# The order of VectorE's state updates and row statistics in the inner cell of an mLSTM step

## The chip, the cores and the metric

The kernel runs on one core of a Trainium2 chip. The metric is the device time of one execution in microseconds. It was run three times as it stood before; the median is 2390.78 us (2387.2 to 2397.85).

## The reference

One step of a two-layer decoder: layer 0 is sliding-window attention, layer 1 an mLSTM block in chunkwise form. The change touches only the chunkwise cell of layer 1, for one head and one chunk of the prompt:

```python
def step(carry, xs):
    C, n, m = carry                       # C (512, 512) per head
    ...
    s = jnp.einsum('bthd,bjhd->btjh', qc, kc) * w_intra
    num = jnp.einsum('btjh,bjhd->bthd', s, vc) + w_inter[..., None] * jnp.einsum('bthd,bhde->bthe', qc, C)
    den = jnp.sum(s, axis=2) + w_inter * jnp.einsum('bthd,bhd->bth', qc, n)
    h = num / jnp.maximum(jnp.abs(den), jnp.exp(-m_t))[..., None]
    ...
    C_new = decay[..., None, None] * C + jnp.einsum('bjhd,bjhe->bhde', kc * wk[..., None], vc)
# after the scan, per token and head:
mu = jnp.mean(h_cell, axis=-1, keepdims=True)
var = jnp.mean(jnp.square(h_cell - mu), axis=-1, keepdims=True)
h_norm = (h_cell - mu) * lax.rsqrt(var + EPS)
```

There are 4 heads of width 512. The prompt has 16 + 1024 tokens, which this kernel cuts into one chunk of 16 and eight of 128 rows. A sample group of 8 sequences with 4 tokens each goes through the same cell as a tenth chunk, and each sequence has a 512 x 512 state of its own.

## The kernel before

The program is written engine by engine: each engine has its own list of instructions in a fixed order, and semaphores hold the lists together. The work of one head in the cell is written by `cell_sp`, `cell_gp`, `cell_pe`, `cell_act` and `cell_dve`. The helper `heads` writes head 0 and head 3 out and runs heads 1 and 2 as two turns of a hardware loop, in which some waits compare with a register. So the same source line has slightly other spacings in heads 1 and 2 than in heads 0 and 3.

For each prompt chunk c (0 to 8) TensorE does, in this order (`cell_pe`):

1. the numerator: queries times the old state C (L1635), a one-column product for the denominator (L1638) and, interleaved with them from chunk 2 on, the four state products of one sample sequence (L1591); then scores times values (L1641, L1646); it then signals `small_ready`;
2. the four 128 x 512 tiles of the new state's product K^T V, three matmuls each (L1653). They go to two PSUM banks in turn, so tile 0 and tile 1 can be made at once, tile 2 waits until VectorE has taken tile 0 into the state (`c_done`), and tile 3 until it has taken tile 1;
3. transposes of the next chunk's keys and values and the next scores (`pre(c + 1)`: L1564, L1570), and a sample numerator (L1601);
4. `back(c)`: the transposes of the normalised output `hb` (L1582), which wait for `h_done(c)` from VectorE. The next chunk's numerator stands behind them and also waits for `sw_done(c + 1)`, VectorE's product of the next scores and weights (L1796).

VectorE (`cell_dve`) does, from `small_ready` on: the denominator (L1943, L1853 to L1855), two state updates, the row statistics of the numerator (`statistics`: L1860, L1861, L1862, the last of which signals `var`), the other two state updates (L1872; L1870 in chunk 0), `normed` (L1879, L1880), which signals `h_done`, the next scores (L1796) and a small update. ScalarE turns the variance into 1/sqrt in two small operations (`norm`: L1745, L1747) and then converts the next chunk's keys and values (`turned`: L1722, L1724). `normed` waits for the second of the small operations (`h_rstd`). These are the functions in question:

```python
done(dve.bn_stats(x[:, 2:8], numerator(c)))                      # statistics(c)
done(dve.bn_aggr(x[:, 8:10], x[:, 2:8]))
dve.tensor_scalar(x[:, 10:11], x[:, 9:10], x[:, 1:2], x[:, 1:2], ALU.mult, ALU.mult).then_inc(sem("var"), 1)
...
dve.wait_ge(sem("u_ready"), due(NU * h + u + 1))                 # prompt_state(c, k)
ins = dve.scalar_tensor_tensor(cst[:, k, :], cst[:, k, :], hbc[:, 1, c:c + 1], U, ALU.mult, ALU.add)
ins.then_inc(sem("c_done"), 1)
...
dve.wait_ge(sem("h_rstd"), due(NCH * h + c + 1))                 # normed(c)
```

In chunk 8 there is no next chunk: after its tiles TensorE does a sample numerator and the four state products of the last sample sequence (L1591), of which the third waits for a VectorE update (L1811) that stands behind `normed(8)` and a copy (L1956). Behind them come `back(8)`, VectorE's gating (L1890), GpSimd's and ScalarE's part of it (L1506, L1752, L1513), and then the output projection (L1678).

Of the kernel before, what the change touches and what calls it, by code (L numbers as in the profile page):

```python
# [97 lines left out]
def due(n):  # L98

    n = n.v if isinstance(n, Idx) else n  # L100
    return max(n, 0) if isinstance(n, int) else n
# [31 lines left out]
def build(nc, a, o):  # L133
# [3 lines left out]
    def sem(name):  # L137
        if name not in sems:
            sems[name] = nc.alloc_semaphore(name + sem_suffix[0])
        return sems[name]  # L140
# [1172 lines left out]
    def u_tile(c, k):  # L1313

        return 4 * c + k if c < 2 else 8 * c - 4 + k
# [465 lines left out]
    def cell_dve(dve, h):  # L1781
        step = [0]

        def done(ins):

            ins.then_inc(sem("cell_step"), 1)
            step[0] += 1
            wait_apart(dve, sem("cell_step"), CELL_STEPS * h + step[0])

        def scores(c):  # L1790
            n, r = ROWN[c], c % 2
            W = sws if c == NCH - 1 else swb[r]
            m = SR if c == NCH - 1 else n
            dve.wait_ge(sem("s_done"), due(NCH * h + pre_no(c) + 1))
            dve.wait_ge(sem("w_done"), due(NCH * h + pre_no(c) + 1))
            dve.tensor_tensor(W[0:m, 0:n], S_[0:m, 0:n], W[0:m, 0:n], ALU.mult).then_inc(sem("sw_done"), 1)  # L1796
# [10 lines left out]
        def sample_state(b, k):  # L1807

            u = u_samp(b, k)
            dve.wait_ge(sem("u_ready"), due(NU * h + u + 1))  # L1810
            dve.scalar_tensor_tensor(scs[b % 2][:, k, :], scs[b % 2][:, k, :], hbc[:, 1, NP + b:NP + b + 1], U_[u % 2],  # L1811
                                     ALU.mult, ALU.add).then_inc(sem("c_done"), 1)

        def key_low(c):

            n, r = ROWN[c], c % 2
            dve.wait_ge(sem("kv_ev"), due(2 * NCH * h + 2 * pre_no(c) + 1))
            dve.scalar_tensor_tensor(kl[r][0:n, :], KT_[0:n, :], hcol[0:n, c, 1:2], kh[r][0:n, :].bitcast(F32),
                                     ALU.mult, ALU.subtract).then_inc(sem("kv_lo"), 1)

        def value_low(c):

            n, r = ROWN[c], c % 2
            dve.wait_ge(sem("kv_ev"), due(2 * NCH * h + 2 * pre_no(c) + 2))
            dve.tensor_tensor(vl[r][0:n, :], VT_[0:n, :], vh[r][0:n, :].bitcast(F32), ALU.subtract).then_inc(sem("kv_lo"), 1)

        def score_low(c):

            n, r = ROWN[c], c % 2
            dve.wait_ge(sem("sw_hi"), due(NP * h + c + 1))  # L1830
            dve.tensor_tensor(swl[r][0:n, 0:n], swb[r][0:n, 0:n], swh[r][0:n, 0:n].bitcast(F32), ALU.subtract)\
                .then_inc(sem("sw_lo"), 1)

        def key_state(c):

            dve.wait_ge(sem("ns_ready"), due(NP * h + c + 1))
            if c == 0:
                ins = dve.tensor_copy(nst[:, :], nsum[0][:, :])
            else:
                ins = dve.scalar_tensor_tensor(nst[:, :], nst[:, :], hbc[:, 1, c:c + 1], nsum[c % 2][:, :], ALU.mult, ALU.add)  # L1840
            ins.then_inc(sem("nst_done"), 1)

        def small(z):
            dve.wait_ge(sem("small_ready"), due(NZ * h + z + 1))

        def numerator(c):
            return pm[0][0:ROWN[c], :]


        def denominator(c):  # L1850
            n, r = ROWN[c], c % 2
            x = cs[0:n, r, :]
            done(dve.scalar_tensor_tensor(x[:, 1:2], x[:, 0:1], -1.0, x[:, 0:1], ALU.mult, ALU.max))  # L1853
            done(dve.tensor_tensor(x[:, 1:2], x[:, 1:2], hcol[0:n, c, 2:3], ALU.max))
            dve.reciprocal(x[:, 1:2], x[:, 1:2])  # L1855

        def statistics(c):
            n, r = ROWN[c], c % 2
            x = cs[0:n, r, :]
            done(dve.bn_stats(x[:, 2:8], numerator(c)))  # L1860
            done(dve.bn_aggr(x[:, 8:10], x[:, 2:8]))  # L1861
            dve.tensor_scalar(x[:, 10:11], x[:, 9:10], x[:, 1:2], x[:, 1:2], ALU.mult, ALU.mult).then_inc(sem("var"), 1)  # L1862

        def prompt_state(c, k):

            u = u_tile(c, k)
            dve.wait_ge(sem("u_ready"), due(NU * h + u + 1))
            U = U_[u % 2]
            if c == 0:
                ins = dve.tensor_copy(cst[:, k, :], U)  # L1870
            else:
                ins = dve.scalar_tensor_tensor(cst[:, k, :], cst[:, k, :], hbc[:, 1, c:c + 1], U, ALU.mult, ALU.add)  # L1872
            ins.then_inc(sem("c_done"), 1)

        def normed(c):
            n, r = ROWN[c], c % 2
            x = cs[0:n, r, :]
            dve.wait_ge(sem("h_rstd"), due(NCH * h + c + 1))
            done(dve.tensor_tensor(x[:, 11:12], x[:, 10:11], x[:, 1:2], ALU.mult))  # L1879
            dve.tensor_scalar(hb[r][0:n, :], numerator(c), x[:, 8:9], x[:, 11:12], ALU.subtract, ALU.mult)\  # L1880
                .then_inc(sem("h_done"), 1)

        def put(c):

            n, r = ROWN[c], c % 2
            (ga, gb), u = gates_of(c), ub[r]
            wait_gates(dve, h, c)
            dve.wait_ge(sem("ul_done"), due(NCH * h + c - 1))
            dve.wait_ge(sem("h_t"), due(NCH * h + c + 1))
            dve.tensor_tensor(u[:, :, 0:n], pm[1][:, :].rearrange("p (k t) -> p k t", k=4)[:, :, 0:n], ga[:, :, 0:n], ALU.mult)\  # L1890
                .then_inc(sem("u_mul"), 1)

        def w_low(j):
            dve.wait_ge(sem("o_hi"), due(4 * h + j + 1))
            dve.tensor_tensor(wlo[j % 3][:, :], wraw[j % 3][:, :], whi[j % 3][:, :].bitcast(F32), ALU.subtract)\
                .then_inc(sem("o_lo"), 1)
# [28 lines left out]
        for c in range(NP):  # L1925
            n, r = ROWN[c], c % 2
            if c == 0:
                dve.wait_ge(sem("cst_out"), 16 * h)
            if c > 0:
                put(c - 1)  # L1930
            score_low(c)
            value_low(c)
            if c > 1:
                sample_state(c - 2, 0)
                sample_state(c - 2, 1)
            key_low(c)
            if c > 1:
                sample_state(c - 2, 2)
                sample_state(c - 2, 3)
            if 0 < c < 4:  # L1940
                w_low(c - 1)
            small(c + 1)
            done(dve.tensor_copy(cs[0:n, r, 0:1], SM[0:n, 0:1]))  # L1943
            dve.sem_inc(sem("small_read"), 1)
            denominator(c)
            prompt_state(c, 0)
            prompt_state(c, 1)
            statistics(c)
            prompt_state(c, 2)
            prompt_state(c, 3)  # L1950
            normed(c)
            if c + 1 < NP:
                scores(c + 1)
            key_state(c)
# [501 lines left out]
    with nc.Block() as block:  # L2456

        @block.sync
        def _(sp):
            gates_sp(sp)  # L2460
            heads(sp, cell_sp)
            final_sp(sp)

        @block.gpsimd
        def _(gp):
            gates_gp(gp)
            heads(gp, cell_gp)

        @block.tensor
        def _(pe):  # L2470
            gates_pe(pe)
            heads(pe, cell_pe)
            final_pe(pe)

        @block.scalar
        def _(act):
            gates_act(act)
            heads(act, cell_act)

        @block.vector  # L2480
        def _(dve):
            gates_dve(dve)
            heads(dve, cell_dve)
            final_dve(dve)
# [52 lines left out]
```

## Time and profile before

| | before |
|---|---|
| median of 3 runs | 2390.78 us |
| profiled execution, time | 2393.39 us |
| profiled execution, span | 2391.6 us |
| mean granted TensorE clock | 0.936 of 2.4 GHz |
| TensorE busy | 2199.0 us, 92% |
| VectorE busy | 1120.0 us, 47% |
| ScalarE busy | 710.5 us, 30% |
| GpSimd busy | 496.2 us, 21% |

The time of an execution is 1.8 us longer than the span of its instructions. The cell takes four stretches of the span, one a head, of about 120 to 130 us each; in them VectorE is busy for about 80% of the time and TensorE for about 93%. The rows below are times in microseconds from the span's start.

### The profile page before, as it was taken

The page shows a single profiled execution, that of the slowest core. Times are in us where ns is not written, and L with a number is a line of the kernel's source. Part 1 is how long each engine was busy: PE and PEld are TensorE (multiplying, and loading weights), DVE is VectorE, ACT ScalarE, POOL GpSimd, SP SyncE. Part 2 cuts the span into 40 slices and gives each one's busy share as a digit, 9 for nine tenths or more (in the row PEclk, how much of TensorE's full clock was granted, in tenths as well). Part 3 has the DMA queues.
Part 4 walks back from the last instruction along what each step waited for, and adds up shares of the span by engine and source line. Part 5 has one row for each costly group of instructions (what it writes and reads, how often), then busy time and mean ns, then how long its engine had stood idle before and what let it go on. Part 6 is the DMA issues. An engine that isn't in the chain of part 4 may idle for free. (4 is left out here: it accounts for less than half of the span.)

```text
span 2391.6 us, 34739 instructions
## 1 busy us (share of the span) xinstructions
PE 2199.0 (92%) x12991; PEld 1906.4 (80%) x12991; DVE 1120.0 (47%) x1906; ACT 710.5 (30%) x1497; POOL 496.2 (21%) x464
## 2 busy tenths in 40 slices
PE   5999979968999999999999999949998988989987
PEld 4999967736999989998999999846685676667667
DVE  6222247832555305430552245037826844853863
ACT  3015648821123323221332223223303302311320
POOL 3000026610421001100110001014503512521530
PEclk7999969956999999999999999978998998998999
DMA  6621021002422332232223222247753861854651
GB/s 208 79 76 44 27 60 53 1 21 74 139 71 82 110 119 64 74 118 101 64 82 119 93 68 77 103 118 256 244 150 97 251 194 39 251 173 118 212 186 74
DMA packets 304084, 268.43 MB, mean 112 GB/s; under 512 B 57558, under 2 KB 249622, under 8 KB 303843
## 3 DMA queue, kind: packets, MB, share of 16 engines
q1 hardware_dynamic: 290046, 217.48, 30.4%
q10 hardware_dynamic: 13880, 48.77, 6.2%
q8 instruction: 109, 1.79, 0.3%
q14 instruction: 49, 0.40, 0.1%
HBM read 164.75 MB, written 102.40 MB: 112 GB/s over the span
## 5 line engine op out<-in xcount | busy, mean ns | idle before, releaser
L381 DVE TENSOR_TENSOR sb_wlo<-sb_wraw,sb_whi 128x1024 fp32r<-128x1024 f32 x100 | 143.2, 1432 | 278.6 <-ACT sb_whi L376 271.8
L376 ACT ACTIVATE sb_whi<-sb_wraw 128x1024 fp32r<-128x1024 f32 x100 | 105.7, 1058 | 515.3 <-PE ps L397 444.5
L397 PE MATMUL ps<-sb_h1h,sb_whi 128*128 128x360 f32 x1152 | 254.2, 329 | 3.5 <-issue 3.5
L397 PE MATMUL ps<-sb_h1l,sb_whi 128*128 128x360 f32 x1152 | 252.6, 327 | 0.0
L397 PE MATMUL ps<-sb_h1h,sb_wlo 128*128 128x360 f32 x1152 | 252.3, 327 | 0.0
L397 PEld LDWEIGHTS ps<-sb_h1h,sb_whi 128*128 128x128 f32 x1152 | 199.2, 189 | 6.2 <-issue 6.0
L397 PEld LDWEIGHTS ps<-sb_h1h,sb_wlo 128*128 128x128 f32 x1152 | 199.9, 188 | 0.0
L397 PEld LDWEIGHTS ps<-sb_h1l,sb_whi 128*128 128x128 f32 x1152 | 199.6, 189 | 0.0
L949 POOL COPY sb_ctail<-sb_xr 128x3 f32<-128x3 f32 (+1 forms) x16 | 3.0, 186 | 708.7 <-DVE sb_xr L1082 708.7
L1635 PE MATMUL pm<-sb_cst,sb_qs 128*128 128x512 f32 x256 | 138.2, 622 | 0.8 <-issue 0.8
L397 PE MATMUL ps<-sb_hh,sb_whi 128*128 128x360 f32 x480 | 117.3, 353 | 15.2 <-DVE sb_hl L418 12.0
L1055 ACT ACTIVATE sb_st<-ps 128x1080 f32<-128x1080 f32 x48 | 51.4, 1072 | 226.4 <-PE ps L397 220.1
L1811 DVE SCALAR_TENSOR_TENSOR sb_scs<-sb_scs,sb_hbc,ps 128x512 f32<-128x512 f32 x128 | 94.4, 743 | 29.5 <-PE ps L1591 29.4
L397 PE MATMUL ps<-sb_hl,sb_whi 128*128 128x360 f32 x480 | 107.7, 333 | 0.0
L1678 PE MATMUL ps<-sb_uh,sb_whi 128*128 128x360 f32 x384 | 92.8, 337 | 15.6 <-POOL sb_ul L1513 15.6
L397 PE MATMUL ps<-sb_hh,sb_wlo 128*128 128x360 f32 x480 | 107.1, 332 | 0.0
L397 PEld LDWEIGHTS ps<-sb_hh,sb_whi 128*128 128x128 f32 x480 | 85.4, 193 | 24.2 <-issue 9.6
L1638 PEld LDWEIGHTS ps<-sb_nst,sb_qs 128*128 128x128 f32 x256 | 49.4, 193 | 64.2 <-issue 64.2
L1972 DVE TENSOR_TENSOR sb_x1T<-ps,sb_x1T 128x1080 f32<-128x1080 f32 x32 | 41.0, 1282 | 126.3 <-PE ps L1678 126.3
L1678 PE MATMUL ps<-sb_uh,sb_wlo 128*128 128x360 f32 x384 | 91.4, 333 | 0.0
L1678 PE MATMUL ps<-sb_ul,sb_whi 128*128 128x360 f32 x384 | 91.2, 333 | 0.0
L1872 DVE SCALAR_TENSOR_TENSOR sb_cst<-sb_cst,sb_hbc,ps 128x512 f32<-128x512 f32 x128 | 89.4, 740 | 0.6 <-issue 0.6
(394 smaller groups left out, 4726.4 us busy)
## 6 DMA issues: line engine op xcount, KB each, us to landing
sb_scs<-state_mlstm_c SPq DMA_DIRECT2D x32, 1024.0 KB, 5.5
sample_mlstm_c<-sb_scs SPq DMA_DIRECT2D x32, 1024.0 KB, 4.3
sb_wraw<-mlstm_w_in SPq DMA_DIRECT2D x48, 512.0 KB, 3.8
sb_wraw<-swa_w_in SPq DMA_DIRECT2D x20, 512.0 KB, 4.0
scratch_ga<-sb_st ACTq DMA_DIRECT2D x16, 540.0 KB, 2.7
scratch_gb<-sb_st ACTq DMA_DIRECT2D x16, 540.0 KB, 3.7
scratch_v<-sb_st ACTq DMA_DIRECT2D x16, 540.0 KB, 2.7
scratch_q<-sb_st ACTq DMA_DIRECT2D x16, 540.0 KB, 2.7
```

What stands on the lines that cost most here:

```text
L376: act.activation(whi[q][:, :], wraw[q][:, :], ACT.Copy).then_inc(sem("w_hi"), 1)
L381: dve.tensor_tensor(wlo[q][:, :], wraw[q][:, :], whi[q][:, :].bitcast(F32), ALU.subtract)\
L397: last = pe.matmul(ps[s][:, g, 0:GRP], w[:, kk, c * P:(c + 1) * P], x[:, kk, g * GRP:(g + 1) * GRP], start=(kk == 0 and i == 0), stop=(kk ...
L949: gp.tensor_copy(dst[:, 0:CW - 1], x[:, NPR:XPR])
L1055: act.activation(v3(st[b][:, 0, :]), ps[c][:, :, 0:GRP], ACT.Copy, scale=(MD ** -0.5 if i // 4 == 2 else 1.0)).then_inc(sem("qkv_ev"), 1)
L1635: pe.matmul(pm[0][0:n, :], qs[r][:, k, 0:n], cst[:, k, :], start=(k == 0), stop=False)
L1638: pe.matmul(SM[0:n, 0:1], qs[r][:, k, 0:n], nst[:, k:k + 1], start=(k == 0), stop=False)
L1678: last = pe.matmul(ps[i % 2][:, g, 0:GRP], w[:, k, c * P:(c + 1) * P], x[:, k, g * GRP:(g + 1) * GRP], start=(k == 0 and t == 0), stop=(k ...
L1811: dve.scalar_tensor_tensor(scs[b % 2][:, k, :], scs[b % 2][:, k, :], hbc[:, 1, NP + b:NP + b + 1], U_[u % 2], ALU.mult, ALU.add).then_inc( ...
L1872: ins = dve.scalar_tensor_tensor(cst[:, k, :], cst[:, k, :], hbc[:, 1, c:c + 1], U, ALU.mult, ALU.add)
L1972: dve.tensor_tensor(v3(x1T[:, i, :]), ps[i % 2][:, :, 0:GRP], v3(x1T[:, i, :]), ALU.add).then_inc(sem("o_done"), 1)
```

## The change

The third and fourth state updates of a chunk are put ahead of the row statistics. VectorE's list changes in all nine prompt chunks of each of the four heads; nothing is added or left out, and no other engine's list changes. The sample chunk (c = 9) has no state updates there and stays as it is.

```diff
             denominator(c)
             prompt_state(c, 0)
             prompt_state(c, 1)
-            statistics(c)
             prompt_state(c, 2)
             prompt_state(c, 3)
+            statistics(c)
             normed(c)
             if c + 1 < NP:
                 scores(c + 1)
```

## Rows read from the trace of the kernel before

**Rows 1.** The page: busy time, share of the span and instructions of each engine.

```profile
PE 2199.0 (92%) x12991; PEld 1906.4 (80%) x12991; DVE 1120.0 (47%) x1906; ACT 710.5 (30%) x1497; POOL 496.2 (21%) x464
```

**Rows 2.** Chain that ended last, head 2, chunk 4: start, length, what.

```profile
2062.79 0.76 DVE sb_cst L1872
2063.59 1.67 PE ps L1653 x6
...
2067.03 0.99 PE ps L1601 x8
2068.03 0.59 PE pm L1582 x4
```

**Rows 3.** Timeline, head 0, chunk 6: start, length, engine, line, idle before and releaser.

```profile
1703.45 1.39 DVE L1872 SCALAR_TENSOR_TENSOR sb_cst<-sb_cst,sb_hbc,ps 128x512 f32<-128x512 f32 x2
1704.23 0.50 PE L1653 MATMUL ps<-sb_vh,sb_kh 128*128 128x512 f32 x1 [0.23 <-DVE sb_cst L1872]
1704.75 0.69 DVE L1860 BATCH_NORM_STATS2 sb_cs<-pm 128x6 f32<-128x512 f32 x1
1704.80 0.40 PE L1653 MATMUL ps<-sb_vh,sb_kl 128*128 128x512 f32 x1
1705.50 0.39 PE L1653 MATMUL ps<-sb_vh,sb_kl 128*128 128x512 f32 x1
1705.70 0.27 DVE L1862 TENSOR_SCALAR sb_cs<-sb_cs 128x1 f32<-128x1 f32 x1
1707.39 0.81 DVE L1880 TENSOR_SCALAR sb_hb<-pm,sb_cs 128x512 f32<-128x512 f32 x1
1708.59 0.66 PE L1582 MATMUL pm<-sb_ident,sb_hb 128*128 128x128 f32 x4
```

**Rows 4.** One line's instructions (L1872): count, then min/median/max of one in ns.

```profile
L1872 DVE SCALAR_TENSOR_TENSOR sb_cst<-sb_cst,sb_hbc,ps x128: 726/740/749, 1635.9 to 2305.3; 128x512 f32<-128x512 f32 x128
```

**Rows 5.** Timeline, head 0, chunk 0: last matmul of tile 3, its reader, the transposes.

```profile
1624.60 0.62 PE L1653 MATMUL ps<-sb_vh,sb_kl 16*128 16x512 f32 x1
...
1625.26 0.69 DVE L1870 COPY sb_cst<-ps 128x512 f32<-128x512 f32 x1 [0.18 <-PE ps L1653]
...
1628.76 0.60 PE L1582 MATMUL pm<-sb_ident,sb_hb 16*128 16x16 f32 x4
```

**Rows 6.** Timeline, head 0, sample chunk: nothing stands between L1862 and L1879.

```profile
1743.01 0.26 DVE L1862 TENSOR_SCALAR sb_cs<-sb_cs 32x1 f32<-32x1 f32 x1
1743.87 0.15 DVE L1879 TENSOR_TENSOR sb_cs<-sb_cs 32x1 f32<-32x1 f32 x1 [0.60 <-ACT sb_cs L1747]
1744.05 0.80 DVE L1880 TENSOR_SCALAR sb_hb<-pm,sb_cs 32x512 f32<-32x512 f32 x1
```

**Rows 7.** Timeline, head 2 (a turn of the loop), chunk 4.

```profile
2064.11 0.69 DVE L1860 BATCH_NORM_STATS2 sb_cs<-pm 128x6 f32<-128x512 f32 x1
2064.16 0.40 PE L1653 MATMUL ps<-sb_vh,sb_kl 128*128 128x512 f32 x1
2064.87 0.39 PE L1653 MATMUL ps<-sb_vh,sb_kl 128*128 128x512 f32 x1
2065.20 0.27 DVE L1862 TENSOR_SCALAR sb_cs<-sb_cs 128x1 f32<-128x1 f32 x1
2066.96 0.81 DVE L1880 TENSOR_SCALAR sb_hb<-pm,sb_cs 128x512 f32<-128x512 f32 x1
2067.68 0.28 DVE L1796 TENSOR_TENSOR sb_swb<-ps,sb_swb 128x128 f32<-128x128 f32 x1
2068.50 0.30 PEld L1635 LDWEIGHTS pm<-sb_cst,sb_qs 128*128 128x128 f32 x2
```

**Rows 8.** Timeline, head 2, sample chunk.

```profile
2127.70 0.26 DVE L1862 TENSOR_SCALAR sb_cs<-sb_cs 32x1 f32<-32x1 f32 x1
2128.81 0.80 DVE L1880 TENSOR_SCALAR sb_hb<-pm,sb_cs 32x512 f32<-32x512 f32 x1
```

**Rows 9.** Timeline, head 0, chunk 8: last matmul of tile 3, and L1880.

```profile
1731.11 0.39 PE L1653 MATMUL ps<-sb_vh,sb_kl 128*128 128x512 f32 x1
...
1732.98 0.81 DVE L1880 TENSOR_SCALAR sb_hb<-pm,sb_cs 128x512 f32<-128x512 f32 x1
```

**Rows 10.** Timeline, head 0, chunk 2: a long wait ahead of tile 2.

```profile
1651.02 0.50 PE L1653 MATMUL ps<-sb_vh,sb_kh 128*128 128x512 f32 x1 [1.78 <-DVE sb_cst L1872]
```

**Rows 11.** Busy time of each engine, granted clock, DMA, around that wait.

```profile
1651.02:1663.50 12.48, 12.48 (x65) 8.43 (x65) 10.42 (x21) 5.31 (x17) 5.40 (x5) 1.00 0.75 222
```

**Rows 12.** One line's instructions (L1635): min/median/max of one matmul in ns.

```profile
L1635 PE MATMUL pm<-sb_cst,sb_qs x256: 590/592/1222, 1629.3 to 2299.4; 128*128 128x512 f32 x128
```

## The prediction

> **What bounds the kernel now.** I read the page first: TensorE is busy for 92% of the span and VectorE for 47% [rows 1]. That is an average over unlike stages, so it settles nothing for the cell. I then read the chain that ended last inside a head [rows 2]. It is TensorE nearly all the way round a chunk, with one link of VectorE: L1872, the first state update, which releases tile 2. From tile 2 on the chain runs without a hole through tiles 2 and 3, the next chunk's transposes and scores, the sample numerator (L1601) and the output transposes L1582. Last I read the timeline of one chunk to see what stands beside that chain [rows 3]. Let S be the start of the first state update (1703.45). TensorE starts tile 2 at S + 0.78 and L1582 at S + 5.14. VectorE, beside it, is through with L1880, whose end is `h_done`, at 1707.39 + 0.81 = 1708.20, that is S + 4.75. So the row statistics and the normalisation are hidden, but L1582 would have waited for them had they come 0.39 us later. That small slack is what the change spends.
>
> **What each part costs.** No instruction is added. Four things move.
>
> *The two state updates go ahead.* In front of the statistics they must wait for tiles that they found ready before. VectorE is free at S + 1.30, where L1860 starts now. Tile 2's last matmul ends at 1704.80 + 0.40 = 1705.20. A copy that waited for such a matmul began 0.04 us after its end (1624.60 + 0.62 against 1625.26) [rows 5]. So update 2 starts at 1705.24, and VectorE stands for 0.49 us. Tile 3 ends at 1705.50 + 0.39 = 1705.89, so update 3 starts at 1705.93; update 2 holds it no longer, since two updates start 0.65 us apart (1703.45 and 1704.75 for two and the statistics) [rows 3]. These times of TensorE stay as they are: tiles 2 and 3 are released by updates 0 and 1, which do not move.
>
> *The statistics move back.* L1860 starts 0.65 us after update 3, at 1706.58 in place of 1704.75. L1862 starts 0.95 us later, as now (1704.75 to 1705.70): at 1707.53.
>
> *The round through ScalarE comes into the open.* Now it lies under updates 2 and 3. In the sample chunk nothing lies over it, and there L1862's start to L1880's start is 1744.05 - 1743.01 = 1.04 us, 0.60 of it VectorE waiting for L1747 [rows 6]. So L1880 starts at 1708.57 and ends at 1709.38, 1.18 us later than before.
>
> *TensorE's wait.* An update's end released a matmul after 0.04 us (1703.45 + 0.74 against 1704.23) [rows 3, 4]. L1582 then starts at 1709.42 in place of 1708.59: **+0.83 us** a chunk. The slack swallowed the other 0.35. VectorE's next scores and the gating stand behind L1880 on VectorE; the next numerator stands behind L1582 on TensorE, GpSimd and the loads behind the gating. All of them go later with it, so there is nobody who would win it back. The conversions of keys and values, queued on ScalarE behind the two small operations, also go later, by about 1.8 us, but must only be there before the next numerator; by the same spacings they end about 0.4 us ahead of it.
>
> *Heads 1 and 2.* In the loop the spacings are longer. Tile 2 ends at 2064.56, tile 3 at 2065.26, so update 3 starts at 2065.30 and L1860 at 2065.95. L1862 follows after 1.09 (2064.11 to 2065.20), at 2067.04 [rows 7]. The open round is 2128.81 - 2127.70 = 1.11 us [rows 8], so L1880 starts at 2068.15 in place of 2066.96, +1.19. Here the next numerator hangs on another thread: L1796 ended at 2067.96 and L1635's weights were loaded at 2068.50, after the transposes, 0.54 us in which the waits between them were worked off [rows 7]. L1796 follows L1880 at a fixed distance. If these waits are what sets L1635, it comes **+1.19 us** later; if only the transposes do, L1582 shifts from 2068.03 (by the chain [rows 2]) to 2068.15 + 0.81 + 0.04 = 2069.00, about +1.0. I take 1.19, because the load of L1635 stood 0.5 us behind the start of L1582 where in head 0 it needs 0.4, and keep 1.0 for the range.
>
> *Chunk 8.* There the chain runs through VectorE itself: after L1880 come the copy, the last sample updates, the gating and the output projection. No slack stands between. Tile 3 ends at 1731.50, update 3 starts at 1731.54, L1860 at 1732.19, L1862 at 1733.14, L1880 at 1734.18 in place of 1732.98 [rows 9]: **+1.20 us**, in every head.
>
> *Chunk 0.* TensorE's matmuls are slower there (0.62 us in place of 0.40) and it is late itself: tile 3's copy starts at 1625.26, so L1860 would start near 1625.9, L1880 near 1627.9 and end by 1628.7, when L1582 starts at 1628.76 anyway [rows 5]. I count 0, at most 0.1 us a head.
>
> **Sum.** Heads 0 and 3: 7 x 0.83 + 1.20 = 7.0 us each. Heads 1 and 2: 7 x 1.19 + 1.20 = 9.5 us each. Together 33 us. Made against its own time, the profiled execution would go from 2393.4 to 2426.4; the median of the runs lies 2.6 us lower, so I forecast 2424 us, 1.4% slower.
>
> *A rule weighed.* Two updates in a row start 0.65 us apart though one lasts 0.74 [rows 3, 4]: the next starts before the record of the last ends. The Trainium skill (VectorE: DVE Perf Modes, The DRAIN you can't avoid) says that the next operation does not start until the pipe of the last is empty, one that nothing holds excepted; read as 0.74 us from start to start, update 3 and L1860 would come 0.14 us later in each of 32 chunks, and the sum would be 37 us in place of 33. The trace has 0.65, and I go by it.
>
> **Rivals.**
>
> *Only the order's cost, without the wait.* If the tiles were there when VectorE reaches updates 2 and 3, as records of TensorE's ends are modelled and the true ones might come earlier, VectorE would run through: L1860 at S + 2.60, L1880's end at S + 5.40, L1582 0.3 us late in head 0. In heads 1 and 2 L1880 and L1796 would be 0.65 us late. 14 x 0.3 + 14 x 0.65 + 4 x 0.65 make 16 us, 2407 us, slower by 0.7%. Against it: the copy of rows 5 waited until exactly such a modelled end.
>
> *Hidden anyway.* If L1582 waited for something else, say the state load that L1601 needs, the statistics could come 1.2 us later for nothing: 2391 us, no change. It decides if TensorE stands by 0.8 us ahead of L1601. The chain has L1601's 0.99 us and L1582 end to end with what is ahead of them [rows 2], so there is no such hole.
>
> *Faster.* Updates 2 and 3 end 0.65 and 0.6 us earlier. If it were update 3 that TensorE waits for before the next numerator, 32 chunks would give up to 20 us: 2371 us. It decides only if TensorE gets to L1635 before update 3 has ended. It ends now near S + 3.9, and L1635 cannot start before L1582 at S + 5.1, so more than 1.2 us of other work would have to go first. Nothing of that is in the rows.
>
> *The clock falls.* Each chunk gets a second hole in TensorE's work, 0.8 to 1.2 us, beside the 0.23 ahead of tile 2 [rows 3]. A matmul of L1635 takes 592 ns in the median and 1222 ns at the slow end [rows 12], so at the lower of the two levels (1.2 in place of 2.4 GHz) the 12.5 us of TensorE's work in a chunk would take up to 12 us more; one such chunk a head makes 48 us more, 2470 us. Against it: a hole of 1.78 us stood in chunk 2 [rows 10], and the 12.5 us behind it ran at a granted clock of 1.00 [rows 11]. The Trainium skill (TensorE: Matmul & The Clock Gate, What's actually happening) calls the slow clock the default state from which activity releases; by it a chunk with more idle time is nearer to falling back. A milder form is likelier: the hole ahead of the third L1591 in chunk 8 grows by 1.2 us, and the few matmuls after it run slow, some 1 to 3 us over all heads.
>
> **How the numbers follow.** The forecast has 0.88, the cost without the wait 0.04, the fallen clock 0.03, hidden anyway 0.03, faster 0.02. A measurement tells about 0.5%, 12 us, from no change. Slower by more: 0.88 + 0.04 + 0.03 = 0.95; within: 0.03; faster: 0.02. The range goes from 2412 (1.0 in heads 1 and 2, and a third of the rest hidden by something that I don't see, 21 us) to 2438 (0.1 us more from `h_done` to L1582 in every chunk, 3 us; the slow matmuls of chunk 8, 3 us; and the 7 us by which the highest run before lay above the median).
>
> **What would show each step.** In head 0: L1860 starts 3.1 us after the first L1872 in place of 1.3, with L1872's second pair split by waits for L1653 (about 0.5 and 0.05 us); L1879 gets a wait for L1747 of about 0.6 us in all chunks; TensorE gets a wait for L1880 ahead of L1582, 0.8 us, in 28 chunks; a chunk takes 13.6 us in place of 12.8 in heads 0 and 3, and 14.3 in place of 13.1 in heads 1 and 2. The prediction is wrong if L1582 starts without such a wait, or if the wait ahead of tile 2 or in the numerator shrinks by what L1582 gained.

## The result: slower by 1.4%, as forecast

The changed kernel takes 2424.75 us in the median of four runs (2420.54 to 2427.55), the kernel before 2389.02 in the same session. The ratio is 1.0141, with a 95% interval of 1.0109 to 1.0172. A second session gave 2428.39 and 1.0150 (1.0132 to 1.0169). The profiled execution took 2427.55 us, with a span of 2425.7.

The engines' busy time on the page answers to [rows 1]. TensorE's has not changed; the 34 us by which the span grew went into waiting.

```profile
PE 2199.3 (91%) x12991; PEld 1901.6 (78%) x12991; DVE 1136.8 (47%) x1906; ACT 709.5 (29%) x1497; POOL 496.5 (20%) x464
```

The view of TensorE's waits (line waited for, then us in total, times, longest) shows in which wait. Before:

```profile
PE ps L1653 <- DVE sb_cst L1872: 24.8, 32, 2.1
```

After:

```profile
PE ps L1653 <- DVE sb_cst L1872: 31.0, 32, 1.8
PE pm L1582 <- DVE sb_hb L1880: 24.6, 26, 1.1
```

The second line did not exist before the change. The first grew by 6.2 us, and nothing in the prediction speaks of that. The wait of chunk 8's products for L1811 grew from 8.0 to 13.6 us, and that of the output projection (L1678) for GpSimd shrank from 15.6 to 11.7.

The timeline of head 0, chunk 6, answers to [rows 3]:

```profile
1706.24 1.39 DVE L1872 SCALAR_TENSOR_TENSOR sb_cst<-sb_cst,sb_hbc,ps 128x512 f32<-128x512 f32 x2
1707.02 0.50 PE L1653 MATMUL ps<-sb_vh,sb_kh 128*128 128x512 f32 x1 [0.23 <-DVE sb_cst L1872]
1708.03 1.43 DVE L1872 SCALAR_TENSOR_TENSOR sb_cst<-sb_cst,sb_hbc,ps 128x512 f32<-128x512 f32 x2 [0.40 <-PE ps L1653]
1709.38 0.69 DVE L1860 BATCH_NORM_STATS2 sb_cs<-pm 128x6 f32<-128x512 f32 x1
1710.32 0.27 DVE L1862 TENSOR_SCALAR sb_cs<-sb_cs 128x1 f32<-128x1 f32 x1
1711.19 0.16 DVE L1879 TENSOR_TENSOR sb_cs<-sb_cs 128x1 f32<-128x1 f32 x1 [0.60 <-ACT sb_cs L1747]
1711.39 0.81 DVE L1880 TENSOR_SCALAR sb_hb<-pm,sb_cs 128x512 f32<-128x512 f32 x1
1712.25 0.66 PE L1582 MATMUL pm<-sb_ident,sb_hb 128*128 128x128 f32 x4 [0.82 <-DVE sb_hb L1880]
```

Read it with S = 1706.24. Update 2 starts at S + 1.79, after a wait for tile 2. L1860 follows at S + 3.14, where [rows 3] had 1.30. Then come 0.60 us for L1747, L1880 at S + 5.15, and L1582 at S + 6.01 after a wait of 0.82 us. Tile 2 itself starts at S + 0.78, as before.

Head 2, chunk 4, answers to [rows 7]:

```profile
2082.98 1.41 DVE L1872 SCALAR_TENSOR_TENSOR sb_cst<-sb_cst,sb_hbc,ps 128x512 f32<-128x512 f32 x2
2086.14 0.69 DVE L1860 BATCH_NORM_STATS2 sb_cs<-pm 128x6 f32<-128x512 f32 x1
2088.37 0.81 DVE L1880 TENSOR_SCALAR sb_hb<-pm,sb_cs 128x512 f32<-128x512 f32 x1
2089.28 0.63 PE L1582 MATMUL pm<-sb_ident,sb_hb 128*128 128x128 f32 x4 [1.08 <-DVE sb_hb L1880]
2089.91 0.30 PEld L1635 LDWEIGHTS pm<-sb_cst,sb_qs 128*128 128x128 f32 x2 [0.24 <-issue]
```

L1635 starts 6.93 us after S = 2082.98; before it was 2068.50 - 2062.79 = 5.71 [rows 2, 7].

The chain that ended last in this chunk answers to [rows 2]. Behind tiles 2 and 3 it comes back from TensorE to VectorE at update 3 and runs on through L1860 and ScalarE's round to L1880:

```profile
2083.78 1.67 PE ps L1653 x6
...
2085.48 0.06 DVE sb_cst L1872
...
2086.14 0.70 DVE sb_cs L1860
...
2088.37 0.82 DVE sb_hb L1880
...
2089.28 0.63 PE pm L1582 x4
```

Chunk 8 of head 0 answers to [rows 9], and chunk 0 to [rows 5]:

```profile
1734.57 1.39 DVE L1872 SCALAR_TENSOR_TENSOR sb_cst<-sb_cst,sb_hbc,ps 128x512 f32<-128x512 f32 x2
1739.74 0.81 DVE L1880 TENSOR_SCALAR sb_hb<-pm,sb_cs 128x512 f32<-128x512 f32 x1
...
1623.87 0.80 DVE L1880 TENSOR_SCALAR sb_hb<-pm,sb_cs 16x512 f32<-16x512 f32 x1
1624.80 0.60 PE L1582 MATMUL pm<-sb_ident,sb_hb 16*128 16x16 f32 x4
```

Positions in us behind S, each the median over chunks 1 to 7 of heads 0 and 3 / of heads 1 and 2 (for L1582 and L1635 the first matmul of the line):

| kernel | L1860 | L1880 | L1582 | L1635 |
|---|---|---|---|---|
| before | 1.30 / 1.32 | 3.94 / 4.17 | 5.13 / 5.16 | 5.62 / 5.72 |
| changed | 3.15 / 3.16 | 5.16 / 5.38 | 6.02 / 6.29 | 6.52 / 6.93 |

### The profile page after: what moved, and what is told of

Its sections match the earlier page's. It is cut to its first block and busy times, and to the rows that moved or that the text cites. A ratio compares the mean times of both kernels' runs of the same rounds, so it can differ in the third digit from the quotient of the medians.

```text
span 2425.7 us, 34739 instructions
## 1 busy us (share of the span) xinstructions
PE 2199.3 (91%) x12991; PEld 1901.6 (78%) x12991; DVE 1136.8 (47%) x1906; ACT 709.5 (29%) x1497; POOL 496.5 (20%) x464
## 3 DMA queue, kind: packets, MB, share of 16 engines
q8 instruction: 109, 1.79, 0.3%
## 5 line engine op out<-in xcount | busy, mean ns | idle before, releaser
L1635 PE MATMUL pm<-sb_cst,sb_qs 128*128 128x512 f32 x256 | 138.5, 624 | 0.7 <-issue 0.5
L1811 DVE SCALAR_TENSOR_TENSOR sb_scs<-sb_scs,sb_hbc,ps 128x512 f32<-128x512 f32 x128 | 94.6, 744 | 30.4 <-PE ps L1591 30.2
L1506 POOL TENSOR_TENSOR sb_ub<-sb_ub,sb_chga 128x512 f32<-128x512 f32 (+1 forms) x36 | 41.9, 1164 | 297.5 <-DVE sb_ub L1890 297.5
L1678 PE MATMUL ps<-sb_uh,sb_whi 128*128 128x360 f32 x384 | 90.7, 331 | 11.7 <-POOL sb_ul L1513 11.7
L1872 DVE SCALAR_TENSOR_TENSOR sb_cst<-sb_cst,sb_hbc,ps 128x512 f32<-128x512 f32 x128 | 90.9, 744 | 14.5 <-PE ps L1653 13.9
L1745 ACT ACTIVATE sb_cs<-sb_cs,sb_epsc 128x1 f32<-128x1 f32 (+2 forms) x40 | 11.8, 294 | 290.9 <-DVE sb_cs L1862 290.9
```

The costliest lines, as they stand in the source:

```text
L1506: gp.tensor_tensor(u[:, :, 0:n], u[:, :, 0:n], gb[:, :, 0:n], ALU.add).then_inc(sem("u_add"), 1)
L1635: pe.matmul(pm[0][0:n, :], qs[r][:, k, 0:n], cst[:, k, :], start=(k == 0), stop=False)
L1678: last = pe.matmul(ps[i % 2][:, g, 0:GRP], w[:, k, c * P:(c + 1) * P], x[:, k, g * GRP:(g + 1) * GRP], start=(k == 0 and t == 0), stop=(k ...
```

## The experiments

**Two waits, taken apart.** The changed order has two waits that the old one hid: VectorE's for tile 2, and its for ScalarE between L1862 and L1879. Four kernels are without one, the other or both; in the first the round is covered again and nothing is left out.

*Three updates ahead of the statistics instead of four.* Update 3 covers ScalarE's round again, and the wait for tile 2 stays.

```
         prompt_state(c, 2)
-        prompt_state(c, 3)
         statistics(c)
+        prompt_state(c, 3)
         normed(c)
```

> Order: updates 0, 1, 2, statistics, 3. Theory A (the cost is what the end of L1880 overshoots the slack ahead of L1582, and it is made of the waits for tiles 2 and 3 and of the round through ScalarE, which lies open when no update stands behind the statistics): update 3 covers the round again. L1860 starts 2.44 us after the first update, L1862 at 3.39, L1880 at 4.46 in heads 0 and 3, where L1582 comes 0.20 us late; L1880 is 0.52 us late in heads 1 and 2 and in every chunk 8. 14 x 0.20 + 14 x 0.52 + 4 x 0.52 = 12 us slower than before, a third of the change. Rival B (each update put ahead costs the same, half of the change each): 17 to 18 us slower. Rival C (the cost is in what GpSimd's and VectorE's changed phase does to the short VectorE operations, not in the waits): no fixed part, anything from 0 to 10 us.

*The changed kernel without ScalarE's round.* L1879 multiplies the variance in place of the reciprocal root, so it needs nothing from ScalarE, which still computes it. The normalisation's scale is thus left out.

```
-            dve.wait_ge(sem("h_rstd"), ...)
-            done(dve.tensor_tensor(x[:, 11:12], x[:, 10:11], x[:, 1:2], ALU.mult))
+            done(dve.tensor_tensor(x[:, 11:12], x[:, 9:10], x[:, 1:2], ALU.mult))
             dve.tensor_scalar(hb[r][0:n, :], numerator(c), ...).then_inc(sem("h_done"), 1)
+            dve.wait_ge(sem("h_rstd"), ...)
```

> The changed kernel, but normed(c) multiplies by the variance in place of 1/sqrt of it and waits for ScalarE's result only after L1880 (this leaves the rsqrt out of the output). Theory A: the wait of 0.60 us ahead of L1879 goes, the waits for tiles stay. L1880 starts 0.39 us after L1862 in heads 0 and 3 and 0.46 in heads 1 and 2: L1582 is late by 0.22 us in heads 0 and 3, L1880 by 0.53 in heads 1 and 2 and in chunk 8. 14 x 0.22 + 18 x 0.53 = 13 us slower than before. Rival B (the round costs nothing, only the tile waits do): as the change, 33 to 38 us slower. Rival C (phase against GpSimd): no fixed part.

*The changed kernel without the wait for tiles 2 and 3.* In chunks 1 to 8 updates 2 and 3 read the numerator, another region of PSUM of the same size that is long complete, in place of their own tile. TensorE still makes the tiles; the state of those two blocks leaves them out.

```
-            dve.wait_ge(sem("u_ready"), due(NU * h + u + 1))
             U = U_[u % 2]
+            if c > 0 and k > 1:
+                U = numerator(c)
+            else:
+                dve.wait_ge(sem("u_ready"), due(NU * h + u + 1))
```

> The changed kernel, but in chunks 1 to 8 updates 2 and 3 add the numerator's bank in place of their tile's and don't wait for the tile (this leaves half of the state update out); TensorE makes the tiles as before. Theory A: L1860 starts 2.60 us after the first update and L1880 ends at 5.42 in heads 0 and 3, L1582 0.34 us late; L1880 0.68 us late in heads 1 and 2 and 0.67 in chunk 8. 14 x 0.34 + 18 x 0.68 = 17 us slower than before. Rival B (the tile waits are harmless, since VectorE has time): as the change, 33 to 38 us slower.

*The changed kernel without either*, with both of these edits and both parts left out.

> Both at once: no wait for tiles 2 and 3 and no wait for ScalarE's result ahead of L1879 (both leave-outs as in the two runs alone). Theory A: L1880 starts 3.94 us after the first update in heads 0 and 3 and 4.18 in heads 1 and 2, just where it started before the change, so the order costs nothing: 0 us, at most a few us from the phase against GpSimd. Two single effects of 20 and 16 us that add up to the whole of the change. Rival C (GpSimd's phase is a part of the cost that the order makes): 5 to 10 us stay. Rival B: the cost stays at 33 us.

Measured in one session beside the kernel before (2388.37 us); the last row is from the first session. The expectations were +12, +13, +17 and 0. The column before the last adds up rows: 14 chunks of heads 0 and 3 and 14 of heads 1 and 2 by how much later L1635 starts behind S, and 4 times L1880's delay for chunk 8.

| kernel | L1880 | L1635 | by rows | measured, ratio (95%) |
|---|---|---|---|---|
| before | 3.94 / 4.17 | 5.62 / 5.72 | | |
| three ahead | 4.46 / 4.69 | 5.82 / 6.25 | +12 | +16.7, 1.0061 (1.0037 to 1.0085) |
| no round | 4.47 / 4.70 | 6.10 / 6.34 | +18 | +21.4, 1.0075 (1.0050 to 1.0101) |
| no tile wait | 4.63 / 4.86 | 5.99 / 6.47 | +18 | +20.6, 1.0076 (1.0052 to 1.0101) |
| neither | 3.94 / 4.17 | 5.64 / 5.82 | +2 | -0.3, 1.0002 (0.9981 to 1.0022) |
| changed | 5.16 / 5.38 | 6.52 / 6.93 | +34 | +35.7, 1.0141 (1.0109 to 1.0172) |

Without both waits L1880 is back at 3.94 / 4.17 to the hundredth, and the time is that of before. So the order of the four updates costs nothing that this interval of 5 us either way can tell; its two new waits cost the rest. Each alone costs about half: the round 18 us by its ratio, the tile's wait 18 us without the round and 15 us with three updates ahead, and these intervals overlap. L1880 says why: it is 0.53 us late with the tile's wait alone, 0.69 with ScalarE's round alone, and 1.21 with both, in series on one engine. Without the round the loss was 5 us above its expectation by the rows (18 against 13), and the traces say why. L1635 came 0.48 later in heads 0 and 3 though L1582 came only 0.21 later, and in heads 1 and 2 0.62 where L1880 came 0.53 later. What held it is ScalarE: it still does its two operations, as late as in the changed kernel, and only then converts the next chunk's keys and values, for which L1635 also waits. Head 0, chunk 6, without the round:

```profile
1704.69 0.59 ACT L1724 ACTIVATE sb_vh<-ps 128x512 fp32r<-128x512 f32 x1
1705.34 0.30 PEld L1635 LDWEIGHTS pm<-sb_cst,sb_qs 128*128 128x128 f32 x2 [0.31 <-issue]
```

L1724 ends at 1705.28, and the load of L1635 follows in the median 0.07 us behind that end in heads 0 and 3 and 0.18 in heads 1 and 2, with the round left out and in the kernel without either. In all the other kernels it follows 0.4 us or more behind it. The 0.27 and 0.09 us over 14 chunks each are the 5 us. So this kernel takes the round off VectorE and not off ScalarE, and 13 us of its 18 by rows are the tile's wait.

In the kernel without either, four updates stand in a row with nothing to wait for, and L1879 follows L1862 at once:

```profile
1694.67 1.38 DVE L1875 SCALAR_TENSOR_TENSOR sb_cst<-sb_cst,sb_hbc,ps 128x512 f32<-128x512 f32 x2
1695.97 1.40 DVE L1875 SCALAR_TENSOR_TENSOR sb_cst<-sb_cst,sb_hbc,pm 128x512 f32<-128x512 f32 x2
1697.29 0.69 DVE L1860 BATCH_NORM_STATS2 sb_cs<-pm 128x6 f32<-128x512 f32 x1
...
1698.42 0.15 DVE L1881 TENSOR_TENSOR sb_cs<-sb_cs 128x1 f32<-128x1 f32 x1
1698.61 0.81 DVE L1882 TENSOR_SCALAR sb_hb<-pm,sb_cs 128x512 f32<-128x512 f32 x1
```

Four updates took 1697.29 - 1694.67 = 2.62 us, 0.655 each. The prediction weighed a rule on this (the Trainium skill, VectorE: DVE Perf Modes, The DRAIN you can't avoid), which excepts an operation that nothing holds. Read without the exception, as 0.74 from start to start, the four would have taken 2.96; the trace goes with the exception.

With three updates ahead, update 3 stands over ScalarE's round, and the wait for L1747 is gone:

```profile
1702.19 0.75 DVE L1872 SCALAR_TENSOR_TENSOR sb_cst<-sb_cst,sb_hbc,ps 128x512 f32<-128x512 f32 x1 [0.40 <-PE ps L1653]
1702.86 0.69 DVE L1860 BATCH_NORM_STATS2 sb_cs<-pm 128x6 f32<-128x512 f32 x1
1703.99 0.74 DVE L1872 SCALAR_TENSOR_TENSOR sb_cst<-sb_cst,sb_hbc,ps 128x512 f32<-128x512 f32 x1
1704.67 0.16 DVE L1879 TENSOR_TENSOR sb_cs<-sb_cs 128x1 f32<-128x1 f32 x1
```

The traces also show what sets L1635 in heads 1 and 2. Taken chunk by chunk, it starts 1.55 us (median) behind L1880 in four of these kernels (before, three ahead, no tile wait, changed), whatever L1582 does, and 1.64 in the two without the round, where L1724 ends so late. In heads 0 and 3 the distance is 1.68 in the kernel before, where the slack lies, and 1.36 in the changed one, where L1582 waits for L1880 and no slack is left.

**The other direction: statistics ahead of all updates.** If the place of the statistics were a question of finding them hidden, ahead of everything might do too.

```
         denominator(c)
+        statistics(c)
         prompt_state(c, 0)
         prompt_state(c, 1)
         prompt_state(c, 2)
         prompt_state(c, 3)
-        statistics(c)
```

> Order: statistics, updates 0, 1, 2, 3, so the other way round. Theory A (TensorE's tile 2 hangs on update 0, and L1582 on the end of L1880 only when that is late): the statistics' 1.14 us (1.28 in heads 1 and 2) stand ahead of tile 2, the end of L1880 gets slack of about 1 us, and L1582 and the next numerator shift by 1.14 and about 1.15 us in 28 chunks; chunks 8 lose 0.5, chunks 0 about 0.6 us each. 36 us slower than before, with the whole hole ahead of tile 2 and none ahead of L1582. Rival E (the statistics only need to be early, as they feed the longest path): 0 us, or faster.

2449.54 us, ratio 1.0249 (1.0233 to 1.0264), +58 us and not the 36 expected. Every chunk gets a hole of 1.3 to 3.2 us in front of tile 2, because update 0, which releases it, is over a microsecond late. The expectation had that cost. It had no cost for TensorE's clock, and the windows of head 0, chunk 6, show it (busy us and count by engine, then granted clock, DMA share, GB/s). The first window ends before the hole, the second begins behind it:

```profile
1705.00:1709.10 4.10, 4.04 (x18) 2.75 (x18) 3.18 (x6) 1.28 (x8) 3.11 (x3) 1.00 0.72 199
1711.27:1714.27 3.00, 3.00 (x8) 2.32 (x9) 1.52 (x3) 0.00 (x0) 0.00 (x0) 0.53 0.29 69
```

Between them stands the hole:

```profile
1711.27 0.66 PE L1653 MATMUL ps<-sb_vh,sb_kh 128*128 128x512 f32 x1 [2.23 <-DVE sb_cst L1872]
```

The second window ran at the lower of the two levels nearly throughout. There are 13 such falls in chunks 1 to 7 of the four heads, none there in the kernel before. Their missing clock, (1 - granted) summed over windows of 2 us, is 22 us: the size of the miss. The chunks without a fall are as expected: from L1943 to the next L1635 they take 7.5 us in heads 0 and 3 and 7.8 in heads 1 and 2 (8.2 in one), where the kernel before takes 6.4 and 6.7 at its shortest.

**The 5 us nobody forecast.** The wait ahead of tile 2 grew though nothing was moved there. Head 0, chunk 5, of the changed kernel:

```profile
1690.64 0.16 DVE L1943 COPY sb_cs<-ps 128x1 f32<-128x1 f32 x1 [0.18 <-PE pm L1646]
1690.92 1.28 POOL L1480 TENSOR_TENSOR sb_qs<-sb_chin,sb_wnt 128x512 f32<-128x512 f32 x1 [1.17 <-DMA sb_chin<-scratch_v]
1690.95 1.27 DVE L1853 SCALAR_TENSOR_TENSOR sb_cs<-sb_cs 128x1 f32<-128x1 f32 x1 [0.15 <-DVE sb_cs L1943]
```

L1853 works on one element a partition and lasts 0.16 us at its shortest. Here it lasts 1.27 us and ends with GpSimd's operation. Summed over 36 chunks, S comes 6.1 us later behind L1943 than it does there at best in the kernel before, and 11.1 us later in the changed one. To test this, L1853 and L1854 were written in a form with one tensor input and the second operand as a scalar pointer, in the kernel before and in the changed one; nothing is left out.

```
-  done(dve.scalar_tensor_tensor(x[:, 1:2], x[:, 0:1], -1.0, x[:, 0:1], ALU.mult, ALU.max))
-  done(dve.tensor_tensor(x[:, 1:2], x[:, 1:2], hcol[0:n, c, 2:3], ALU.max))
+  done(dve.tensor_scalar(x[:, 1:2], x[:, 0:1], -1.0, x[:, 0:1], ALU.mult, ALU.max))
+  done(dve.tensor_scalar(x[:, 1:2], x[:, 1:2], hcol[0:n, c, 2:3], None, ALU.max))
```

> The kernel before with the same denominator, written so that L1853 and L1854 have one tensor input each (the second operand is taken as a per-partition scalar). In the profiles the two lines now and then last 0.3 to 1.3 us in place of 0.16 and then end 0.01 to 0.02 us after a GpSimd tensor_tensor (L1480) or tensor_scalar (L1498) ends. Theory A (they lose a lock on something that two-input operations of VectorE share with GpSimd): the long ones vanish, the first update starts 0.78 us (0.94 in heads 1 and 2) after L1943 in every chunk, and the 6.1 us that the four heads now lose there are given back: 6 us faster, ratio 0.9975. Rival D (GpSimd's traffic slows any VectorE operation on SBUF): nothing changes, 0 us.

> The same rewriting in the changed kernel. Its profile loses 11.1 us to the long L1853 and L1854. Theory A: 11 us faster than the changed kernel, so about 25 us slower than before in place of 36. Rival D: as the changed kernel, 36 us slower than before.

> The changed kernel once more, beside the other three on one chip: 33 to 38 us slower than before, ratio 1.014 to 1.016. All theories agree; it is the yardstick for the one-input version.

In one session, with the kernel before at 2391.3 us:

| kernel | median us | ratio (95%) |
|---|---|---|
| before, one input | 2384.40 | 0.9971 (0.9959 to 0.9983) |
| changed, one input | 2421.33 | 1.0127 (1.0111 to 1.0142) |
| changed, again | 2428.39 | 1.0150 (1.0132 to 1.0169) |

The form ends the collision. This is the changed kernel with it, at the same place in the chunk:

```profile
1689.80 1.29 POOL L1480 TENSOR_TENSOR sb_qs<-sb_chin,sb_wnt 128x512 f32<-128x512 f32 x1 [1.15 <-DMA sb_chin<-scratch_v]
1689.86 0.21 DVE L1853 TENSOR_SCALAR sb_cs<-sb_cs 128x1 f32<-128x1 f32 x1
```

The wait ahead of tile 2 fell from 31.0 to 25.4 us in the changed kernel. The expected 6 us came, and in the changed kernel 7 of the expected 11. But the end of the collision does not explain them all, and that the first number fits is partly luck. From chunk 1 to chunk 8, summed over the heads, the kernel before went from 377.97 to 376.66 us, only 1.3 less, since each of the new operations costs 0.05 us more, which the expectation had left out. The larger part is in chunk 0 of heads 1 and 2, which went from 17.08 and 17.17 us to 14.80 and 15.10. The 22 matmuls behind the start of the numerator there are the same in both, at another clock. Before, and before with one input:

```profile
1817.16:1824.59 7.43, 7.43 (x22) 4.34 (x23) 3.30 (x4) 2.70 (x12) 6.04 (x6) 0.74 0.70 186
```

```profile
1812.62:1818.17 5.55, 5.55 (x22) 3.49 (x23) 3.23 (x4) 2.76 (x12) 5.22 (x6) 1.00 0.69 186
```

All eight such chunks in four profiles of kernels with the one-input form took 14.7 to 15.1 us. Of the 16 in the other eight profiles, three did; the rest took 15.9 to 17.7. So the gain goes with the form, but why the clock is up there is not shown.

**The version that came out best.** With the one-input form, the maximum and the reciprocal were also moved out of the way of update 0, whose end TensorE waits for.

```
             denominator(c)            # only the absolute value
             prompt_state(c, 0)
             prompt_state(c, 1)
+            denominator_end(c)        # maximum, reciprocal
             statistics(c)
```

> The order of before with the one-input forms of the normalization, and its maximum and reciprocal moved from behind the absolute value to behind the update of tile 1. Nothing is left out. Update 0 then starts two small operations earlier, until the last matmul of tile 0 holds it instead: about 0.7 us after the absolute value in place of 0.86 to 1.0. Theory (the interval to the next chunk's first output counts only as far as the chain through the updates is what ends it): in heads 0 and 3 everything behind update 0 comes 0.15 to 0.19 us earlier, so 16 chunks give 2.5 to 3 us over the one-input kernel, some 2382 us; heads 1 and 2 too by as much if their chain really hangs on the row statistics, as in the changed kernel, then 5 us, some 2379. Rival (the first maximum is the bound at the end of the chunk, by the tile-0 wait): nothing, 2384.

> The order of before with the one-input forms, once more beside its variant with the late maximum: 6 us under before again (2385), if that gain is the kernel's and not the run's.

2380.99 us (ratio 0.9963, 0.9949 to 0.9977) and 2382.39 (0.9971, 0.9955 to 0.9986), with the kernel before at 2389.3. The gain of the one-input form is confirmed. The 1.4 us between the two are less than these intervals can tell. Head 0, chunk 6, with the late maximum (its lines stand 4 lower; L1876 is the update):

```profile
1696.02 1.41 DVE L1876 SCALAR_TENSOR_TENSOR sb_cst<-sb_cst,sb_hbc,ps 128x512 f32<-128x512 f32 x2 [0.24 <-PE ps L1653]
1697.35 0.21 DVE L1858 TENSOR_SCALAR sb_cs<-sb_cs,sb_hcol 128x1 f32<-128x1 f32 x1
```

Update 0 now waits for tile 0's last matmul, as expected. From L1943 to S it is 0.76 / 0.71 us in place of 0.89 / 1.04, and from S to L1635 5.65 / 6.12 in place of 5.62 / 5.72. So heads 0 and 3 win and heads 1 and 2 don't: there the two moved operations delay L1880 by what S gained, and L1635 stays 1.55 behind it. From chunk 1 to chunk 8 the profile is 2.2 us shorter in heads 0 and 3 together and 0.1 in heads 1 and 2, which is the expectation's first case.

## Why the prediction was right

Its steps against the rows of head 0, chunk 6, and head 2, chunk 4, and the medians above:

| step | predicted | measured |
|---|---|---|
| update 2 starts, behind S | 1.79 | 1.79 |
| L1860 | 3.13 / 3.16 | 3.14 / 3.16 |
| wait for L1747 | 0.60 | 0.60 |
| L1880 | 5.12 / 5.36 | 5.15 / 5.39 |
| L1582 | +0.83 / about +1.0 | +0.89 / +1.14 |
| L1635, heads 1 and 2 | +1.19 | +1.21 |
| L1880 in chunk 8, heads 0, 3 / 1, 2 | +1.20 | +1.23 / +1.21 |
| chunk 0, L1582 of heads 0, 3 / 1, 2 | 0 | 0 (S + 7.34 in both) / +0.17 |

*The wait for tile 2* held to the hundredth, and taking it away gave back half of the loss. *ScalarE's round* lasts 1711.39 - 1710.32 = 1.07 us in the open, where the sample chunk said 1.04 [rows 6]. *The slack* of 0.39 us swallowed part of the delay in heads 0 and 3. *In heads 1 and 2* L1635 hangs on L1880, as chosen between 1.0 and 1.19; four kernels show the fixed distance. *The rival without the wait* was run as such. Its 16 us came out as 18, and its L1880 at 4.63 / 4.86 is within 0.04 us of where it put it. *Hidden anyway* and *faster* fall with the wait of 24.6 us for L1880: no other releaser appeared ahead of L1582, and the earlier end of updates 2 and 3 was worth nothing. The ends of the range are 1 us off what their own terms add up to (2411 and 2437 in place of 2412 and 2438), which changes nothing here.

**Where the sum came out right for more than its own reasons.** It had 33 us. The cell, from the first L1943 of head 0 to the last of head 3, grew from 681.25 to 719.52 us, by 38.3:

- heads 0 and 3, 14 x 0.90 = 12.6, and heads 1 and 2, 14 x 1.21 = 16.9: 29.5 us, predicted 28.3;
- S later behind L1943, by L1853 and L1854 held up: +5.0, not in the sum;
- matmuls on a slow clock in two chunks: +3.2 (what is left of chunks 0 to 7), not in the sum;
- from chunk 8 to the next head's chunk 0, three times: +0.6, predicted 3.6.

A chunk from 1 to 8 took 1.24 us longer on average in heads 0 and 3 and 1.42 in heads 1 and 2, where the prediction's sign was +0.8 and +1.2; the rest is L1853, L1854 and the clock.

The stages ahead of the cell were 4.0 us shorter in this profile, and behind its last L1943 0.2, where the last chunk 8 had been given 1.2. Nothing that was changed lies ahead of the cell. So 34 us remain in the span. The two unforeseen costs, 8 us, and the 1.2 by which the chunks came out above their term were hidden in the total by these 4 us and by 4.4 that chunk 8's term did not show. The total fits by luck to that extent.

*Chunk 8* needs its own word, since the term was 4.8 us and the cell shows little of it. The delay does travel: in head 0 L1582 is 1.23 later behind S, and the first L1678, the output projection, comes 1.23, 1.80, 1.81 and 1.30 us later behind chunk 8's L1943 in heads 0 to 3. That is 6.1 us. Further on it can't be followed. The three stretches from chunk 8 to the next head's chunk 0 are 0.6 us longer in this profile and 4.4 in the second profile of the changed kernel, but profiles with the order of before differ by as much (238.6 to 242.9 us for the three). Whether the term is really paid is not shown.

*The clock falls* was given 0.03 and in its mild form placed in chunk 8. There it came in heads 1 and 2, whose L1678 is 1.8 us late in place of 1.2. This is head 1 from the start of L1582 to the first L1678, the same nine matmuls, before and then changed:

```profile
1928.66:1933.86 5.20, 2.44 (x9) 0.75 (x8) 4.17 (x11) 0.98 (x3) 2.52 (x2) 0.98 0.64 191
```

```profile
1945.98:1951.51 5.53, 4.39 (x9) 1.22 (x8) 3.91 (x7) 0.63 (x1) 2.52 (x2) 0.63 0.65 192
```

The change is not its only cause, since head 2 has it too in the order of before with the one-input form (0.56). Two falls came elsewhere, in head 1, chunk 3, and in head 0 behind the same hole ahead of tile 2 in chunk 2 that had been the argument against them [rows 10, 11]. In the changed kernel:

```profile
1648.85:1650.00 1.15, 1.15 (x4) 0.94 (x5) 0.73 (x2) 0.00 (x0) 0.00 (x0) 0.85 0.36 134
1650.00:1653.00 3.00, 3.00 (x13) 2.64 (x12) 2.40 (x5) 0.00 (x0) 0.00 (x0) 0.50 0.70 159
```

The hole is 1.78 us in both, and in the changed kernel a hole of 0.81 us stands ahead of L1582 in the chunk before it. But that second hole does not decide. In head 3 of the same profile the same pair is followed by no fall:

```profile
2241.33 0.66 PE L1582 MATMUL pm<-sb_ident,sb_hb 128*128 128x128 f32 x4 [0.81 <-DVE sb_hb L1880]
...
2251.34 0.50 PE L1653 MATMUL ps<-sb_vh,sb_kh 128*128 128x512 f32 x1 [1.79 <-DVE sb_cst L1872]
...
2252.00:2262.00 10.00, 9.18 (x52) 5.92 (x51) 8.02 (x16) 4.65 (x14) 3.62 (x4) 1.00 0.84 242
```

And the kernel without either wait, which has no such second hole, falls in head 0, chunk 3, behind a hole of 1.85 us, where the kernel before has one of 1.87 and no fall:

```profile
1655.40 0.50 PE L1653 MATMUL ps<-sb_vh,sb_kh 128*128 128x512 f32 x1 [1.85 <-DVE sb_cst L1875]
...
1657.00:1660.00 3.00, 3.00 (x15) 2.95 (x14) 2.26 (x6) 1.48 (x4) 0.00 (x0) 0.50 0.63 203
```

So the inference from one long hole without a fall to none in the changed kernel was too strong: the same holes go either way, and what decides stays open. The size was small: these two falls are 3.4 us of missing clock.

## What to carry to other kernels

On an in-order engine, ask of each operation that is moved forward whether its input is there yet, and of what is moved back what it used to stand over: here both answers were waits of about half a microsecond, in series, and a slack of 0.4 us was spent with them. When a total agrees with a forecast, still check its terms, since a single profile moves by several us with the level of TensorE's clock in stages that the change doesn't touch. And when a wait is taken away to price it, look at who else hangs on the engine that was waited for: here ScalarE's conversions still came late and cost 5 of the 18 us.

## What the runs showed of the hardware that was not expected

**A tiny VectorE operation waits for a large GpSimd one.** L1853 and L1854 take two tensor inputs from SBUF (in L1853 the same column twice) and write one element a partition. Beside L1480 or L1513 on GpSimd they lasted up to 1.27 us in place of 0.16, and ended within 0.02 us of GpSimd's operation. Beside L1498 L1853 lasted 0.34 to 0.35 us and ended 0.86 us ahead of it. All instances of L1853, with minimum, median and maximum in ns, in the changed kernel and in the kernel before with one input:

```profile
L1853 DVE SCALAR_TENSOR_TENSOR sb_cs<-sb_cs x40: 146/342/1266, 1616.5 to 2349.7; 128x1 f32<-128x1 f32 x32, 16x1 f32<-16x1 f32 x4, 32x1 f32<-32x1 f32 x4
```

```profile
L1853 DVE TENSOR_SCALAR sb_cs<-sb_cs x40: 195/214/216, 1617.4 to 2306.4; 128x1 f32<-128x1 f32 x32, 16x1 f32<-16x1 f32 x4, 32x1 f32<-32x1 f32 x4
```

The Trainium skill (SBUF — State Buffer, Who interferes with whom) says that a VectorE instruction with two SBUF inputs contends with a GpSimd instruction that reads SBUF, and one with at most one such input doesn't; by that rule, both rows agree. The cost is not in the size of the operation but in that of its neighbour. That the changed order meets it more often goes with its longer chunks, in which GpSimd's L1480, released by a load, falls on another moment of VectorE's; this was only argued.

**TensorE's clock does not follow the lengths of the holes alone.** One hole of 1.78 us had no fall behind it; a pair of 0.8 and 1.8 us had one in head 0 and none in head 3 of the same profile; a hole of 1.85 us had a fall in one kernel where 1.87 had none in another; and 13 falls came in 28 chunks that each had a hole of 1.3 to 3.2 us. What makes chunk 0 of heads 1 and 2 run at either level, 2.2 us apart, stays open.
